# One stage for the output projection, the norm behind it and the first queries, in a one-core decoder layer

## The reference, cut to what matters

```python
mix = (sigmoid(gate_a) * (A @ w_pa) + sigmoid(gate_b) * (B @ w_pb)) @ w_o
x   = LN(alpha * x + gate_m * mix)
ff  = PEER(x * (1 + scale_f) + shift_f)      # queries q = h @ peer_wq, then experts
x   = LN(alpha * x + gate_f * ff)
```

## Time and profile before

| | |
|---|---|
| median of 3 runs | 4198.99 us (4197.4 to 4199.7) |
| the profiled execution | 4198.86 us, span 4196.7 us |
| TensorE busy | 3518.9 us, 84% |
| VectorE busy | 2454.0 us, 58% |
| GpSimd busy | 1486.2 us, 35% |
| ScalarE busy | 944.4 us, 23% |

### The profile page before, as it was taken

One profiled execution on the slowest core, in us unless ns is written; L12 is line 12 of the kernel. 1 busy time (PEld: TensorE's weight loads), 2 busy tenths in 40 slices (PEclk: granted clock), 3 DMA queues, 4 the chain that ended last, 5 costly groups with the idle time before them and its releaser, 6 DMA issues. The chain is left out here.

```text
span 4196.7 us, 58323 instructions
## 1 busy us (share of the span) xinstructions
PE 3518.9 (84%) x22278; PEld 2528.6 (60%) x22278; DVE 2454.0 (58%) x5133; ACT 944.4 (23%) x1396; POOL 1486.2 (35%) x1269
## 2 busy tenths in 40 slices
PE   6997999977878859888889899977677777878997
PEld 3665676744555849776767676755455554545566
DVE  3364222235213340799989999998666666664445
ACT  2121111102222132232232232322111111111222
POOL 0001111100000103044455565646566666664530
PEclk8998999987989979899999999988899899999999
DMA  5000111015012234588899999979999999999992
GB/s 196 31 20 27 33 32 33 32 60 198 30 43 110 94 125 138 162 289 286 292 339 375 332 379 352 393 286 337 385 393 398 376 398 397 397 380 383 394 344 91
DMA packets 370234, 982.03 MB, mean 234 GB/s; under 512 B 37073, under 2 KB 136601, under 8 KB 361008
## 3 DMA queue, kind: packets, MB, share of 16 engines
q0 software_dynamic: 150912, 549.52, 34.4%
q1 hardware_dynamic: 219056, 428.83, 28.8%
HBM read 867.45 MB, written 110.78 MB: 233 GB/s over the span
## 5 line engine op out<-in xcount | busy, mean ns | idle before, releaser
L1918 POOL DMA_INDIRECT u_rows<-in_u_rows,idx_u x512 | 671.0, 1310 | 785.7 <-DVE dots L1956 584.2
L1929 POOL DMA_INDIRECT v_rows<-in_v,idx_v x512 | 630.9, 1232 | 258.9 <-issue 143.4
L1956 DVE CUSTOM_DVE_ANT_0 u_rows<-u_rows,x_rows 128x1024 f32<-128x1024 f32 x512 | 619.8, 1221 | 152.1 <-DMA u_rows<-in_u_rows,idx_u 120.4
L2366 PE MATMUL hid_ps<-dh,u_high 128*128 128x512 f32 x1152 | 477.0, 414 | 74.8 <-DVE u_low L2618 41.7
L2366 PE MATMUL hid_ps<-dl,u_high 128*128 128x512 f32 x1152 | 472.4, 410 | 0.0
L2366 PE MATMUL hid_ps<-dh,u_low 128*128 128x512 f32 x1152 | 470.2, 408 | 0.0
L2015 PE MATMUL ff_ps<-v_rows,diag 128*8 128x512 f32 x2048 | 266.8, 642 | 74.1 <-DMA v_rows<-in_v,idx_v 70.2
L2366 PEld LDWEIGHTS hid_ps<-dh,u_high 128*128 128x128 f32 x1152 | 226.3, 196 | 139.9 <-DVE u_low L2618 65.5
L2824 ACT ACTIVATE dh<-v_raw 128x1024 fp32r<-128x1024 f32 x128 | 135.3, 1057 | 729.9 <-DMA v_raw<-in_v 550.9
L2879 PE MATMUL turn_ps<-w_high,dh 128*128 128x512 f32 x384 | 171.0, 445 | 147.8 <-DVEq L2961 108.9
L716 PE MATMUL side_ps_scan<-h,w_side_scan 128*128 128x344 f32 x768 | 270.7, 479 | 0.3
(11 more groups left out here) (434 smaller groups left out, 6387.4 us busy)
## 6 DMA issues: line engine op xcount, KB each, us to landing
u_raw<-in_u SPq DMA_DIRECT2D x128, 512.0 KB, 6.7
v_raw<-in_v SPq DMA_DIRECT2D x128, 512.0 KB, 11.4
hidden_saved<-hid SPq DMA_DIRECT2D x128, 256.0 KB, 6.8
gates_saved<-gates SPq DMA_DIRECT2D x32, 1024.0 KB, 7.6
hidden_back<-hidden_saved SPq DMA_DIRECT2D x128, 256.0 KB, 13.9
g_back<-gates_saved SPq DMA_DIRECT2D x60, 320.0 KB, 16.5
x<-in_w_ada SPq DMA_DIRECT2D x16, 1024.0 KB, 8.1
g_back<-gates_saved SPq DMA_DIRECT2D x30, 384.0 KB, 19.7
```

Source lines behind the costliest of these rows:

```text
L1918: self.nc.gpsimd.indirect_dma_start(self.u[:, n % RU], None, self.io["u_rows"], bass.IndirectOffsetOnAxis(ap=index, axis=axis)).then_inc(l ...
L1929: self.nc.gpsimd.indirect_dma_start(self.v[:, n % RV], None, self.io["v"], bass.IndirectOffsetOnAxis(ap=index, axis=0)).then_inc(self.v_la ...
L1956: V.tensor_tensor_reduce(self.u[:, n % RU], self.u[:, n % RU], self.xt[:], 1.0, 0.0, ALU.mult, ALU.add, accum_out=self.dots[:, i % 2, k:k ...
L2366: mm = nc.tensor.matmul(ps[b % 2][:], u[:, b % RING, k], h[:, k], start=at == 0, stop=at == 3 * KD - 1)
```

## The change

`merge` asks for `x` right behind the first two sets of weights and gates, loads all of `w_o` in its middle, into the space of the mixer's input, and GpSimd multiplies `x` by `ALPHA` there. `mixer_output`, `layernorm` and `peer_queries` become one block, `output_and_queries`. It goes over four tiles of tokens, 256 wide (the third has the 8 samples too, and the third and fourth change places so that the samples come earlier). For each tile TensorE runs the 8 blocks of `w_o` from SBUF; the mean of tile j-1 stands behind its third block, the variance behind its sixth, and transposes behind its second and fourth. VectorE joins each block with `x` straight from PSUM, and makes the low parts of `w_o`. `h_peer` stays in SBUF, in the space of `mh`; the split sparse operands take the space of `ml` and `mh`, `dh` and `dl` that of `x`. The first two query blocks are interleaved with the last tile's norm. The order of PE's list after the last tile is `query(0,0)`, mean, `query(1,0)`, variance, `query(0,1)`, `query(1,1)`, the samples' transpose, then blocks 2 to 15.

```diff
         with ExitStack() as tokens:
             env["x"] = sb(tokens, "x", [P, KD, T])
+            x_at = nc.sbuf_base - KD * T * 4
...
+                env["wo_raw"] = nc.alloc_sbuf_tensor_at("wo_raw", [P, KD, KD, P], F32, offset=h_at)
+                env["wo_low"] = nc.alloc_sbuf_tensor_at("wo_low", [P, KD, KD, P], F32R, offset=h_at)
...
+                env["hf"] = nc.alloc_sbuf_tensor_at("h_peer", [P, KD, T], F32, offset=nc.sbuf_base - 2 * KD * T * 4)
                 merge(**env)
-                mixer_output(**env)
-            with ExitStack() as l1:
-                env["h"] = sb(l1, "h_peer", [P, KD, T])
-                layernorm(**env, name="1", modulate=(SC_F, SH_F))
-        del env["x"], env["h"]
-        with ExitStack() as pr:
-            for n in ("dh", "dl"):
-                env[n] = sb(pr, n, [P, KD, TDN], F32R)
-            peer_queries(**env)
+                for s, n in enumerate(("dh", "dl")):
+                    env[n] = nc.alloc_sbuf_tensor_at(n, [P, KD, TDN], F32R, offset=x_at + s * KD * TDN * 4)
+                output_and_queries(**env)
+            del env["h"]
+            pr = tokens.enter_context(ExitStack())
             env["sparse"] = Sparse(nc, io, sb, pb, sems, pr, consts)
...
+                for m in range(KD):
+                    s = m % 2
+                    sp.wait_ge(w_free, m + 2)
+                    sp.dma_start(w[:, s].rearrange("p q k n -> p (q k n)"), io["w_merge"][m].rearrange("p k n -> p (k n)"))\
+                        .then_inc(w_loaded[s], 16)
+                    sp.dma_start(gate[:, s], io["side_saved"][:, 2 * m + 6:2 * m + 8, :]).then_inc(g_loaded[s], 16)
+                    if m == 1:
+                        sp.dma_start(x[:], io["x_saved"]).then_inc(x_back, 16)
+                    if m in (2, 3, 4, 5):
+                        for n in (2 * m - 4, 2 * m - 3):
+                            sp.dma_start(wo_raw[:, n], io["w_o"][n]).then_inc(wo_loaded, 16)
+                sp.wait_ge(wo_loaded, 16 * KD + 1)
+                sp.wait_ge(x_scaled, KD + 1)
...
+            def _(pool):
+                pool.wait_ge(x_back, 17)
+                for k in range(KD):
+                    nc.gpsimd.tensor_scalar(x[:, k], x[:, k], ALPHA, None, ALU.mult).then_inc(x_scaled, 1)
...
+TILES = ((0, 256), (256, 256), (768, 256 + NS), (512, 256))
+PROMPT = 256
+HOME = (0, 256, TS + 256, TS)
...
+        sh, sl = ml[:, :, 0:TS], mh[:, :, 0:TS]
...
+                for n in range(4):
+                    load(n)
+                for j in range(2):
+                    store_x(j)
+                    store_rows(2 * j)
+                    store_rows(2 * j + 1)
+                store_x(2)
+                store_x(3)
                 for n in range(COUNT):
-                    if n + 2 < COUNT:
-                        load(n + 2)
-                    if n <= SAMPLES:
-                        at, size = members(n)
-                        sp.wait_ge(row_taken, 2 * n + 2)
-                        sp.dma_start(io["h_rows"][at:at + size], rows[0:size, n % 2].rearrange("p k n -> p (k n)"))\
-                            .then_inc(row_stored[n % 2], 16)
-                    sp.wait_ge(taken, n + 1)
+                    if n + 4 < COUNT:
+                        load(n + 4)
...
+                    sp.wait_ge(q_taken, n + 1)
                     sp.dma_start(io["query_saved"][n, :, 0:TS], out[:, n % 2]).then_inc(q_stored[n % 2], 16)
...
+                def project(j, n):
+                    at, size = TILES[j]
+                    b = j * KD + n
+                    if j == 0:
+                        pe.wait_ge(o_low, n + 1)
+                    if b >= 4:
+                        pe.wait_ge(joined, b - 3)
+                    for k in range(KD):
+                        for q, (w, v) in enumerate(((wo_high[:, n], mh), (wo_high[:, n], ml), (wo_low[:, n], mh))):
+                            mm = nc.tensor.matmul(ps[b % 4 // 2][:, b % 2, 0:size], w[:, k], v[:, k, at:at + size],
+                                                  start=k == 0 and q == 0, stop=k == KD - 1 and q == 2)
+                    mm.then_inc(o_summed, 1)
+
+                def mean(j):
...
+                    pe.wait_ge(joined, (j + 1) * KD)
+                    if j:
+                        pe.wait_ge(centred, j)
+                    for k in range(KD):
+                        mm = nc.tensor.matmul(mean_ps[:, 0:size], col(consts, "mean"), tile(j)[:, k], start=k == 0, stop=k == KD - 1)
+                    mm.then_inc(mean_summed, 1)
...
+                    pe.wait_ge(squared, j + 1)
+                    if j:
+                        pe.wait_ge(rooted, j)
+                    for k in range(KD):
+                        mm = nc.tensor.matmul(var_ps[:, 0:size], col(consts, "mean"), square(j)[:, k], start=k == 0, stop=k == KD - 1)
+                    mm.then_inc(var_summed, 1)
...
+                    if i < SAMPLES:
+                        pe.wait_ge(modulated, (i // 2 + 1) * KD)
+                    else:
+                        pe.wait_ge(samples_ready, 1)
...
+                def query(n, t):
+                    tok = slice(t * QT, (t + 1) * QT)
+                    if n < 2:
+                        pe.wait_ge(joined, 3 * KD + 5 + 2 * n + t)
+                        pe.wait_ge(s_low, 2 + t)
+                    else:
+                        pe.wait_ge(q_taken, n - 1)
+                    pe.wait_ge(w_low, n + 1)
...
+                for j in range(len(TILES)):
+                    for n in range(KD):
+                        project(j, n)
+                        if j and n == 2:
+                            mean(j - 1)
+                        if j and n == 5:
+                            variance(j - 1)
+                        if j >= 2 and n in (1, 3):
+                            turn(2 * (j - 2) + n // 2)
+                for n, t in STEPS:
+                    query(n, t)
+                    if (n, t) == (0, 0):
+                        mean(3)
+                    if (n, t) == (1, 0):
+                        variance(3)
+                    if (n, t) == (1, 1):
+                        turn(SAMPLES)
...
                 def high(n):
                     act.wait_ge(w_loaded[n % 2], 16 * (n // 2 + 1))
                     if n >= 2:
-                        act.wait_ge(summed, n - 1)
+                        act.wait_ge(q_summed, n - 1)
                     S.activation(wh[:, n % 2], raw[:, n % 2], ACT.Copy).then_inc(w_high, 1)
...
+                def square_tile(j):
+                    act.wait_ge(centred, j + 1)
+                    S.activation(square(j), tile(j), ACT.Square).then_inc(squared, 1)
...
+                def root(j):
+                    act.wait_ge(var_summed, j + 1)
+                    if j >= 2:
+                        act.wait_ge(multiplied, j - 1)
+                    S.activation(rstd[:, j % 2, 0:TILES[j][1]], var_ps[:, 0:TILES[j][1]], ACT.Sqrt, bias=col(consts, "ln_eps"))\
+                        .then_inc(rooted, 1)
+
+                def modulate(j):
+                    at = TILES[j][0]
+                    for k in range(KD):
+                        act.wait_ge(scaled, j * KD + k + 1)
+                        S.activation(hf[:, k, HOME[j]:HOME[j] + PROMPT], x[:, k, at:at + PROMPT], ACT.Identity,
+                                     scale=mod[:, SC_F + k, 0:1], bias=mod[:, SH_F + k, 0:1]).then_inc(modulated, 1)
...
+                        act.wait_ge(row_stored[i % 2], 16 * (i // 2))
+                    for f in range(2):
+                        act.wait_ge(row_turned, 2 * i + f + 1)
+                        S.activation(rows[0:size, i % 2, f * HALF:(f + 1) * HALF], row_ps[f][0:size], ACT.Copy).then_inc(row_taken, 1)
+
+                for n in range(KD):
+                    S.activation(wo_high[:, n], wo_raw[:, n], ACT.Copy).then_inc(o_high, 1)
                 high(0)
+                high(1)
+                for j in range(1, len(TILES)):
+                    if j >= 2:
+                        turned_rows(2 * (j - 2))
+                        turned_rows(2 * (j - 2) + 1)
+                    square_tile(j - 1)
+                    root(j - 1)
+                    modulate(j - 1)
+                    if j < 3:
+                        act.wait_ge(modulated, j * KD)
+                        S.activation(sh[:, :, (j - 1) * 256:j * 256], hf[:, :, (j - 1) * 256:j * 256], ACT.Copy).then_inc(s_high, 1)
+                act.wait_ge(o_summed, len(TILES) * KD)
+                act.wait_ge(samples_ready, 1)
+                S.activation(sh[:, :, TSP:TS], hsm[:], ACT.Copy).then_inc(s_high, 1)
+                square_tile(3)
+                root(3)
+                modulate(3)
                 for n in range(COUNT):
-                    if n + 1 < COUNT:
-                        high(n + 1)
-                    act.wait_ge(summed, n + 1)
+                    if n + 2 < COUNT:
+                        high(n + 2)
+                    act.wait_ge(q_summed, n + 1)
```

(64 more changed lines are left out.)

296 lines of the change are left out of this document (81 added, 215 removed).

## The result

Four executions of the changed kernel took 4154.28, 4151.53, 4148.81 and 4140.06 us, median 4150.17 us; four of the kernel before, beside them, 4199.34 us. The ratio is 0.9874, 95% interval 0.9861 to 0.9888. The forecast was 4149, range 4139 to 4161.

What follows compares the result with a forecast made beforehand. Queries bound by TensorE; norm and reload by a chain of dependent steps. 2.6 + 92.6 + 28.2 + 96.8 + 1.7 + 6.1 + 2.4 + 1.5 = 231.9 us, saving 50 from 4198.9: 4149 us, range 4139 to 4161.

Steps and rivals of the forecast that it cites:

- 1624: End of the new stage: the last copy of queries starts at about 1624 us, against 1674.0 before.
- the 2.6 us to the first product: Stage start: one ScalarE rounding 1.06, one VectorE subtraction 1.22 and handing over 0.3 before the first w_o matmul.
- the ports: First tile of w_o: VectorE's and GpSimd's subtractions collide on shared SBUF ports, 1.5 us, bounds 0 and 3.
- 92.6 + 28.2 + 96.8: TensorE's work in us: w_o's products, the norm's means and sums of squares, then queries and turns.
- Rival (c): w_o's smaller tiles: stationary loads limit matmuls to 188 ns, 144 us in place of 92.6, total 4200; chance 0.03.
- (b): Less waiting: faster modulations, no clock fall, no port collision; 4138 to 4143 us; chance 0.10.
- Rival (a): Tiles of w_o: less hidden than thought, three tiles lose 2 to 4 us each; 4156 to 4163; chance 0.13.
- The margins worked out for square and variance: Centring and square take 4.4 us against 8.4 of cover in tile 1; 2.4 us to spare in tiles 2 and 3.
- The waits behind w_o: TensorE waits 1.7 us before the last variance and 6.1 before the third query weight's matmuls.
- 2.4 for the clock: After the 6.1 us wait the granted clock is 0.50 for 4.80 us, costing another 2.4 us.
- Rival (e): Later stages: the gain is given back because one is paced by something that doesn't move up; within 0.2%; chance 0.01.
- Rival (d): New stage: short waits keep the clock at 0.50; w_o alone adds 88 us, 4237; chance 0.03.

Runs made afterwards that it cites:

- three edits in a row: In turn: third query weight rounded early, stage 226.9 us; half query before variance, fourth early, 230.2; loads before x's last store, 223.9; changed kernel 232.2.
- the serial norm: Changed kernel with all of w_o first, then the norm of all tiles in its own order, nothing reloaded: stage 254.7 us against 232.2, ratio 0.9926.

## Why the prediction was right

**The result and the method.** From the start of the stage the prediction went to 1624, 234.7 us behind the last subtraction of `merge`; measured are 232.2. The 2.5 us too many: 0.5 in the stage's start (its first rounding comes 1.9 us after `merge`'s last subtraction, where I had taken the 2.4 of before), 0.2 in the 2.6 us to the first product (2.4), 1.0 in the ports, 0.4 in rounding 1623.6 up, and 0.4 in all the other terms.

**TensorE's work.** 92.6 + 28.2 + 96.8 with the waits and the clock, 229.3 us from the first product to the last copy; measured 227.9 (1400.2 to 1628.1), and with the ports at 0.5 the sum would be 228.3. That matmuls go by columns held: a group of 256 columns, 24 matmuls, comes every 2.84 us, 0.118 us each, against 188 ns of the LDWEIGHTS record. Rival (c) is out. Two sums of the rivals are off without effect: w_o alone at the low clock adds 91 us by the prediction's own 90.6, not 88 (4240, not 4237), and the terms of (b) lead down to 4139, not 4138.

**No wait in tiles 1 to 3.** Held: 113.56 busy of 113.70 us. Rival (a) is out by the same row. The margins worked out for square and variance held: 4.0 us in tile 1, where the square ends at 1441.3 and the variance starts at 1445.4, and 2.4 in tiles 2 and 3, where 3.2 and 2.9 are measured. For tile 2 these are the rows:

```profile
1472.16 1.92 ACT L1738 ACTIVATE h_peer<-x 128x2048 f32<-128x2048 f32 x1
```
```profile
L1676 PE MATMUL var_ps<-h_peer,consts x16: 378/379/380, 1477.3 to 1480.5; 128*128 128x256 f32 x16
```

The thinnest margin was one that the prediction hadn't worked out, the 2.2 us between the last modulation and the first turn. That it was enough is partly luck.

**The waits behind w_o.** 1.7 forecast, 1.4 measured; 6.1 forecast, 6.0 measured; 2.4 for the clock; half of the 4.7 us at 0.50 is 2.35, and the distances of the matmuls give 2.2. The cause named, the rounding behind eight modulations in ScalarE's order, is shown by the version that moves it, and the clock's part by the matmuls that fill the wait. What I did not see is what comes next: the rounding of the fourth weight behind the same modulations, and the load of the fifth behind the store of `x`. In the changed kernel both cost nothing, as the wait before the third block covers them.

**The mis-sized term** is the shared ports: 1.5 us priced, 0.5 measured. The prediction gave each of two subtractions a slack of 0.8 us and still charged 1.5 us. Measured, they took 1.99 and 2.48 us and not 1.22, 0.8 and 1.3 more; less the slack that leaves 0 and 0.5, which is what the run with the engines apart gives. GpSimd's second subtraction was held up too, 3.39 us against 2.40 at most when apart. The Trainium skill, "SBUF — State Buffer", section "SBUF: two separate sides", calls the shared ports an exclusive lock for the whole instruction, and by it I had put the wait at up to 3 us. The lengthened instructions on both engines agree with a lock; the 3 us of wait are not there. A bound was wrong too, without effect: GpSimd's eight scalings of `x` take 2.86 us each and not at most 2.39, by one row of the groups by line:

```profile
L1485 POOL TENSOR_SCALAR x<-x 128x1032 f32<-128x1032 f32 x8 | 22.7, 2860 | 97.6 <-DMA x<-x_saved 97.6
```

These instructions lie in `merge` with nobody behind them. The loads that were moved there cost nothing that can be seen: `merge` takes 106.4 us with and without those of w_o.

**Luck.** That the median, 4150.17, lies at 4149 is partly chance: against the kernel before beside it, the change saved 49.2 us here, 46.2 and 53.0 in the two other sets of runs. The stage gave 2.5 us more than I forecast, and the profiled execution had lost 6.6 us ahead of it. I had no term for such losses: single executions of the changed kernel took 4140.06 to 4162.03 us, with a stage that was 232.2 us in all three profiles.

**The rest of the kernel.** Rival (e) is out: from the last copy to the end are 2524.4 us, against 2522.7 before, and 2523.5 and 2521.0 in the two other profiles of the change. Over all profiles it is 2514.7 to 2535.9, a spread of the later stages that follows no edit here and that I have not traced. Rival (b) is out too, as both waits and the slow clock behind the second came as forecast; only its part on the ports was near.

**Rival (d)**, the slow clock throughout, is out: the granted clock is 1.00 over 113.7 us in which no wait of PE reaches 1 us.

## What to carry to other kernels

When a stage is a chain of small steps between two stages of full matmul work, put the steps between the matmuls by tiles, and write out for each step how many us of matmul cover it and how much is to spare: the sum held to 1%, and the two steps without cover were exactly the waits that the trace showed. Do it for each pair of steps that hands over to TensorE, as the thinnest margin can be one that isn't on the list. Look behind each wait that you remove for the instruction that is late next, on the DMA queue's list too: here three edits in a row were needed for 8.8 us, and the second, without the third, gave back 3.3 of the 5.3 us that the first had won. And where whole executions spread by more than the effect, measure between two instructions that both kernels share.

## What was unexpected in the hardware

- The granted clock in unchanged code differed from one execution to the next: 1.00, 0.89 or 0.83 from 30 to 60 us; the stage behind it started 2 to 7 us later at the two lower ones.
- A wait of 6.0 us was followed by 4.7 us at 0.50, one of 5.4 us by 5.0 or more, two of 9.3 us by 5.0 and 5.3. Waits of 1.4 us left it at 1.00, but in the serial norm two of 2.5 us, with 3.7 us of matmuls between them, were followed by 3.4 us at 0.50. Short matmuls whose sum isn't used kept it at 1.00.
- At 0.50 the matmuls of 260 columns came 0.217 us apart, 1.8 times their 0.120 us at 1.00, so 4.7 us at 0.50 cost 2.2 and not 2.35.
- The steady query blocks took 5.73 us each in ten of the fourteen profiles and 5.77 in four, in one and the same code and at a clock of 1.00.
- GpSimd's multiplication of one fp32 operand by a constant, 128x1032, took 2.84 us in the median, longer than its subtraction of two, 128x1024, with a median of 2.39.
